# The context tokens' retention gate is computed in the selection stage instead of the output stage

## The reference, cut to what matters

```python
def mixer(h, ...):
    q, k, v, g_ret, cb, cc, cx, ga, gb = jnp.split(h @ w_in, SPLIT_POINTS, axis=-1)
    ...
    y_ret = (jax.nn.silu(g_ret) * o) @ w_ret_o
    u = short_conv3(cc * cx, conv_w)
    y_conv = (cb * u) @ w_conv_o
    merged = jax.nn.sigmoid(ga) * y_ret + jax.nn.sigmoid(gb) * y_conv
    return merged @ w_o, s_f, s_b

def expert_choice_ffn(h, w_router, w_gate, w_up, w_down):
    aff = jax.nn.softmax((hf @ w_router).astype(jnp.float32), axis=-1)
    vals, idx = lax.top_k(aff.T, cap)              # 128 latents, 16 context tokens for each expert
    xs = hf[idx]
    hid = jax.nn.silu(xs @ w_gate) * (xs @ w_up)
    out = (hid @ w_down) * vals                    # added to the rows idx

def trunk_layer(x, cond, ...):
    h = rmsnorm(x, n_pre_mix) * (1.0 + sc1) + sh1
    m, s_f, s_b = mixer(h, ...)
    x = x + g1 * rmsnorm(m, n_post_mix)
    h = rmsnorm(x, n_pre_ffn) * (1.0 + sc2) + sh2
    f = expert_choice_ffn(h, ...)
    return x + g2 * rmsnorm(f, n_post_ffn), s_f, s_b
```

## Time and profile before

| What | Value |
|---|---|
| median of 3 runs | 2033.02 us (2032.63 to 2034.11) |
| the profiled execution's own time | 2034.96 us |
| its span | 2033.2 us |
| mean granted TensorE clock | 0.994 |
| busy share of the span | PE 98%, PEld 83%, DVE 57%, ACT 37%, POOL 13% |

### The profile page before, as it was taken

How to read it: one execution, slowest core, us unless ns; L and a number is a source line. 1 busy time by engine, 2 the same in 40 slices (tenths; PEclk the granted TensorE clock), 3 DMA queues, 4 the chain that set the end, 5 groups by cost and what they waited for, 6 DMA issues and landing times.

```text
span 2033.2 us, 32674 instructions
## 1 busy us (share of the span) xinstructions
PE 1987.5 (98%) x12723; PEld 1694.8 (83%) x12723; DVE 1168.4 (57%) x1621; ACT 753.6 (37%) x869; POOL 272.8 (13%) x277
## 2 busy tenths in 40 slices
PE   6999999999999999999999999999999999999995
PEld 4898989899999999999888888777777777777774
DVE  5654545476554232232223648877777777777766
ACT  7622222231111112111112332655556555555555
POOL 1010101011002000000000122111211111112215
PEclk9999999999999999999999999999999999999998
DMA  9011111225554311112334757788887778888888
GB/s 337 26 53 47 42 46 44 90 83 159 152 152 161 104 33 52 41 32 62 103 93 161 271 180 261 297 318 317 311 310 297 273 299 318 316 316 317 305 312 231
DMA packets 189577, 372.32 MB, mean 183 GB/s; under 512 B 11836, under 2 KB 110132, under 8 KB 188628
## 3 DMA queue, kind: packets, MB, share of 16 engines
q1 hardware_dynamic: 170304, 312.30, 42.4%
q0 software_dynamic: 19120, 59.29, 9.7%
q10 hardware_dynamic: 100, 0.03, 0.0%
HBM read 326.98 MB, written 43.03 MB: 182 GB/s over the span
## 4 chain that ended last, share of the span: by engine, by line
PE 82%; issue 7%; DVE 5%; POOL 2%; DMA 2%; ACT 2%; SPq 0%; POOLq 0%; DVEq 0%; ACTq 0%
PE ps L1436 8%; PE ps L1418 8%; PE ps L1073 8%; PE ps L1074 8%; PE ps L1075 8%; PE ps L1420 8%; PE ps L1427 8%; PE ps L1119 3%; PE ps L1120 3%; PE ps L1121 3%; PE ps L1085 2%; PE ps L1087 2%; PE ps L1086 2%; PE ps L1168 1%; PE ps L1169 1%
## 5 line engine op out<-in xcount | busy, mean ns | idle before, releaser
L2547 DVE TENSOR_TENSOR e_lo<-raw,e_hi 128x2048 fp32r<-128x2048 f32 x192 | 439.2, 2289 | 88.6 <-ACT e_hi L1913 88.6
L1913 ACT CAST e_hi<-raw 128x2048 fp32r<-128x2048 f32 x192 | 367.3, 1913 | 210.8 <-PE ps L1427 209.3
L1073 PE MATMUL ps<-h_hi,w_hi 128*128 128x384 f32 x744 | 249.4, 335 | 0.0
L1074 PE MATMUL ps<-h_lo,w_hi 128*128 128x384 f32 x744 | 248.5, 334 | 0.0
L1075 PE MATMUL ps<-h_hi,w_lo 128*128 128x384 f32 x744 | 248.5, 334 | 0.0
L2100 DVE TENSOR_TENSOR w_lo<-w_raw,w_hi 128x1024 fp32r<-128x1024 f32 x64 | 79.3, 1239 | 192.5 <-ACT w_hi L1612 192.4
L1418 PE MATMUL ps<-e_hi,x_hi 128*128 128x512 f32 x512 | 160.0, 394 | 0.7 <-DVE e_lo L2547 0.4
L1420 PE MATMUL ps<-e_lo,x_hi 128*128 128x512 f32 x512 | 157.8, 389 | 0.0
L1073 PEld LDWEIGHTS ps<-h_hi,w_hi 128*128 128x128 f32 x744 | 139.6, 188 | 3.3 <-issue 3.3
L1074 PEld LDWEIGHTS ps<-h_lo,w_hi 128*128 128x128 f32 x744 | 139.6, 188 | 0.0
L1075 PEld LDWEIGHTS ps<-h_hi,w_lo 128*128 128x128 f32 x744 | 139.6, 188 | 0.0
(11 more groups left out here) (359 smaller groups left out, 3721.2 us busy)
## 6 DMA issues: line engine op xcount, KB each, us to landing
raw<-in_w_gate_dram SPq DMA_DIRECT2D x64, 1024.0 KB, 8.4
raw<-in_w_up_dram SPq DMA_DIRECT2D x64, 1024.0 KB, 13.2
raw<-in_w_down_dram SPq DMA_DIRECT2D x64, 1024.0 KB, 9.6
w_raw<-in_w_in_dram SPq DMA_DIRECT2D x48, 512.0 KB, 4.1
ada_k<-in_w_ada_dram SPq DMA_DIRECT2D x32, 512.0 KB, 5.0
ada<-in_w_ada_dram SPq DMA_DIRECT2D x7, 1024.0 KB, 16.5
merged_d<-merged POOLq DMA_DIRECT2D x8, 576.0 KB, 6.2
ffn_d<-zero POOLq DMA_DIRECT2D x9, 512.0 KB, 7.0
```

The lines of the kernel that those rows point to most:

```text
L1073: pe.matmul(out, w_hi[:, slot, k, :], xh, start=(k == 0), stop=False)
L1074: pe.matmul(out, w_hi[:, slot, k, :], xl, start=False, stop=False)
L1913: act.copy(e_hi[u % 4][:].rearrange("p k n -> p (k n)"), raw[(u + 8) % 12][:].rearrange("p k n -> p (k n)"))\
L2547: dve.tensor_tensor(e_lo[u % 4][:].rearrange("p k n -> p (k n)"), raw[(u + 8) % 12][:].rearrange("p k n -> p (k n)"), e_hi[u % 4][:].rearr ...
```

## The change

- ret_out's gate product is made for latents alone: two blocks of 512 tokens in place of three of 384. The context part of `gate` is filled with 1.0 once, so that w_ret_o's product is stored unscaled for the context.
- CTX_UNITS grows from 8 to 12: units 8 to 11 are the context's ga, in plain float32, with ACT's sigmoid (`sig_ga`) and one more multiplication on POOL. SP loads four more pieces of weights of 1 MB for them. The 22 dummy matmuls go.
- mix_context is cut in pieces: 24 matmuls, 12 matmuls, then 6 and 6 around the flip of the choice.
- DVE's select order: the two m_lo_c subtractions come after rounds 12 and 15 instead of 6 and 8.
- The scaling by the root and by g1, the addition of the input, and the second norm's scaling are now on DVE, behind the first two units of the first expert. h2's transpose, the routing and the choice of the context stand between later units.
- In first_expert TensorE does down units 8 and 9 before the context's units 0 to 7, and the hidden transposes before both.
- SP holds units 3 to 7 of the first expert until the gather of the latents has landed (before, units 5 to 7).
- POOL issues the gather before it makes the context's two roots.

```diff
-CTX_SLOT = [8, 11, 9, 10, 8, 11, 9, 10]
+CTX_SLOT = [8, 11, 9, 10] * 3
...
+            for j in range(4, 8):
+                sp.wait_ge(projected, ctx_made(j))
+                load_ctx(j + 4)
...
+            sp.wait_ge(m_made, NT)
             sp.wait_ge(got_l, 16)
-            for u in range(5, 8):
+            for u in range(3, 8):
                 load_unit(0, u, True)
...
             pool.wait_ge(sel_read, 1)
             gather_latents(0)
+            m_deviation(8, 0)
+            x1_deviation(8, 0)
...
-                for b in range(NB):
+                for b in range(2):
+                    ts = slice(CTX + HALF * b, CTX + HALF * b + HALF)
...
-                    project(T_RETOUT + 2 * n, 0, h_hi, h_lo)
+                    project_latents(T_RETOUT + 2 * n, 0, h_hi, h_lo)
...
-            mix_context(0)
-            mix_context(1)
-            keep_busy(6, 22)
+            pe.wait_ge(act_evicted, EA_CONVOUT + KD + 5)
+            pe.wait_ge(m_lo_done, NT)
+            mix_context(range(0, 4), range(2))
+            pe.wait_ge(m_lo_done, NT + 1)
+            mix_context(range(4, 8), range(1))
...
+            dve.wait_ge(z_lo_done, KD)
+            did(dve.memset(gate[:, 0:CTX], 1.0))
...
-            for half, rounds in enumerate((range(6), range(6, 8))):
+            for half, rounds in enumerate((range(12), range(12, 15))):
...
             def first_expert():
-                dve.wait_ge(ctx_scaled, 2)
-                did(dve.tensor_tensor(h2_own[:], h2_own[:], scale_c[:], ALU.mult))
-                settle()
-                dve.tensor_tensor(h2_own[:], h2_own[:], shift_c[:], ALU.add).then_inc(h2_ready, 1)
                 low(0, 0)
                 low(0, 1)
+                dve.wait_ge(m_rstd, NT)
+                dve.scalar_tensor_tensor(x1_c[:].rearrange("p (a n) -> p a n", a=2), ps[:, 0:2, :], stats[:, 8:9],
+                                         g1_c[:].rearrange("p (a n) -> p a n", a=2), ALU.mult, ALU.mult).then_inc(ctx_scaled, 1)
+                dve.wait_ge(ctx_scaled, 1)
+                dve.wait_ge(xr_in[0], 16 * 5)
+                dve.tensor_tensor(x1_c[:], x1_c[:], x_res_c[:], ALU.add).then_inc(x1_ready, 1)
+                low_rows(0)
+                dve.wait_ge(x1_rstd, NT)
+                dve.scalar_tensor_tensor(h2_own[:], x1_c[:], stats[:, 12:13], scale_c[:], ALU.mult, ALU.mult).then_inc(ctx_scaled, 1)
...
+                low(0, 2)
+                low(0, 3)
+                low(0, 4)
                 top_logit(8)
-                low_rows(0)
+                low(0, 5)
                 affinities(8)
```

More of the change, by code:

```diff
@@ L912, in gather_context @@
                     .then_inc(got_c, 16)
-            pool.wait_ge(m_in[0], 16 * 5)
             for half in range(2):
@@ L1452, in first_expert @@
                         pe.transpose(ps[0:CAP_C, 4, 144:160], sel_f[0:EXPERTS, CAP_L:CAP], id16).then_inc(sel_turned, 1)
[L1453 to L1455 removed]
+                pe.wait_ge(sel_copied, 2)
+                pe.matmul(ps[:, 7, 0:2 * EXPERTS], flip[0:CAP_C, P:2 * P], sel_c[:], start=True, stop=True).then_inc(sel_flipped, 1)
+                for half in range(2):
+                    turn_hidden(half, half + 1)
+                turn_rows(1)
+                down(0, 8)
+                down(0, 9)
                 pe.wait_ge(xc_turned, 1)
```

167 lines of the change are left out of this document (82 added, 85 removed).

## The result

| | before | changed kernel |
|---|---|---|
| median of 20 runs each | 2032.64 us (2030.79 to 2034.37) | 2036.07 us (2033.76 to 2037.64, but for one of 4044.86) |
| the profiled execution's own time | 2034.96 us | 2035.98 us |
| its span | 2033.2 us | 2034.2 us |
| ratio of the runs | 1 | 1.0015, 95% interval 1.0009 to 1.0022 |

The changed kernel is 3.4 us slower, where 1.5 us less than the old median of 2033.02 was forecast. 2036.07 lies in the range of 2026 to 2037.5, but the sign is wrong, and the interval excludes no change. In the profiles the difference is only 1.0 us, since the profiled execution of before (2034.96) was a long one for its kernel. The experiments show where most of that comes from.

A forecast was written before the change was run, and what follows sets the result against it. TensorE, busy 98% of the span, was taken as the bound. The terms -11.3 + 1.0 + 0.1 + 7.2 + 1.5 gave -1.5 us, so 2031.5 us from a median of 2033.02, range 2026 to 2037.5.

The forecast's parts named there:

- Turns 2 to 8 of the retention: Retention's output stage: the gate product in the new form saves 1.61 us a turn, 11.3 us over seven turns.
- The lower bound: Smallest saving for retention turns 2 to 8 if time goes by columns alone: 7 x 1.3 = 9.1 us.
- The first turn: First retention turn: later output transposes delay VectorE, which ends the turn, so it loses 1.0 us.
- The start of the first expert: Selection to first expert: the gathered rows' transposes start where they do now, at 1282.35, so the start moves +0.1 us.
- the 4 us of ctx units that stick out: Selection: of the added 14.46 us of ctx units on TensorE, 4 us exceed the cover of 11.7.
- The gather: POOL's gather beside VectorE's two-input units stands still until unit 0 ends; its rows land at 1282.35.
- The first expert: Context work moved between its units adds 8.4 us, less 1.2 of present waits: 7.2 us more, ends 4 and 10.
- the clock (+1.5): First expert: after a 3.3 us pause, units 0 and 1 meet the lower clock, costing 0.8 to 2.4, taken as 1.5 us.
- The second fall of the clock: Rival: the 2.4 us pause before unit 7 brings half clock there: +2.9, 2034.4 us, chance 0.15.
- The held units: Rival: first expert's held weights arrive together, unit 3 at about 1296 instead of 1287.5: 2038 us, chance 0.12.
- The ctx units' loads: Rival: the selection's four added weight loads are not hidden, TensorE waits up to 3.7 us: 2035 us, chance 0.06.
- signs of being wrong: First expert under 52 us, gate's form saving less than 1.3 us a turn, or unit 3 landing late.

The follow-up runs named there:

- e3: The changed kernel with 7 dummy matmuls before TensorE's wait for the adaLN rows in the first retention turn: median 2035.13 us, ratio 1.0006 to the kernel before.
- e10: The changed kernel with the last output transposes placed earlier between the first turn's gate matmuls, no dummies there: median 2032.64 us, ratio 0.9998 to the kernel before.
- e1: The kernel before, unchanged, profiled a second time: profiled execution 2037.32 us, median 2033.67 us.
- e15: The kernel before, unchanged, profiled a third time: one execution of 2034.0 us.
- e5: e3 with VectorE's context scaling and addition moved in front of the low parts of units 0 and 1: 2034.58 us, ratio 1.0010 to the kernel before.
- e14: e13 with unit 0's low part made during VectorE's wait for the choice's turn, context scaling and addition before unit 1's: median 2029.51 us, ratio 0.9980 to before.
- e8: e3 with unit 7's low part before the context's choice, and the choice's flip between the hidden transposes: median 2032.40 us, ratio 0.9998 to the kernel before.
- e13: The changed kernel with e10's earlier transposes and e8's unit 7 order, no dummies added: median 2031.37 us, ratio 0.9989 to the kernel before.
- e2: The changed kernel, unchanged, profiled a second time: profiled execution 2034.92 us, median 2035.89 us.
- e16: The changed kernel, unchanged, profiled a third time: one execution of 2037.66 us.
- e7: e3 with units 3 and 4 loaded before the gather lands, only 5 to 7 held: median of 9 runs 2037.68 us, ratio 1.0028 to the kernel before.
- e12: The kernel before with 26 dummies instead of 22 under the choice in the selection: median 2032.20 us, ratio 0.9995 to the kernel before.
- e4: The kernel before with only the retention's gate product changed to latents, context's gate left out: median of 5 runs 2023.89 us, ratio 0.9954 to the kernel before.

## Why the prediction was wrong, step by step

- **Turns 2 to 8 of the retention (-11.3).** Right in kind, 1.55 us a turn instead of 1.61: -10.85, which misses by 0.4. The lower bound has a slip: by columns alone the saving is 12.49 - 11.10 = 1.39 us a turn, 9.7 over seven, not 1.3 and 9.1. The measured value lies between the bounds all the same.
- **The first turn (+1.0).** The mechanism was right (transposes late, VectorE late, the turn ends with VectorE) and measures +1.26. The step that failed is what was left out beside it: the price of TensorE's pause, put at nothing without a reason. Both halves of TensorE's wait stood in the text, 1.6 us less product and 1.0 more of VectorE, but they were not added up to a pause of 2.6 us. The text asked what a pause of that length does to the clock in the selection, and not here. The pause was 3.24 us, and the fall behind it costs 1.6 to 1.7 (e3, e10). In place of +1.0 the term is +3.0 where the clock falls, as it did in 3 profiles of 3.
- **The start of the first expert (+0.1).** This is the second step that failed. The term agrees with the first profile, and that is the trap. "A clock of 0.52 where only dummies ran" was taken as free, but the dummies stood in front of the routing, and the 6.24 us of them had set the 1282.35 against which the new rows were compared. Against the usual 47.4 us the changed kernel's 49.0 is +1.6. So the forecast's base held 1.5 us of a fall that was longer in this one of three profiles, and the term was subtracted from a median. That the median's executions mostly have the short fall is not shown; e1 and e15 speak for it. (In the working up to here, the 4 us of ctx units that stick out are 3.3 by the prediction's own rows; its 1272.4 is added up separately and fits: the choice's transposes came 0.9 us later behind the selection's start than before, with 0.7 forecast.)
- **The gather.** Held as forecast (2.48 us, 1.07 when VectorE is idle). The Trainium skill's rule ("GPSIMD Engine Reference", section Specifications), that POOL's memory interface is shared with VectorE and a VectorE instruction with two inputs there gets in its way, agrees with e5 and e14, and with the 0.99 us of the earlier trace rows beside x_lo, a subtraction that takes one of its two inputs from TensorE's output ps.
- **The first expert (+7.2) and the clock (+1.5).** Together 8.7, measured 8.56. TensorE waits 2.47 us for unit 7 (forecast 2.4), 2.17 for the hidden rows and unit 8 (2.4), 0.30 for unit 9 (0.8). But the agreement of the sum is luck. A low clock over units 0 and 1 costs nothing (e8, e13, e14, and e2), since VectorE and the landing of the held weights set unit 7's start; the forecast subtracted only the 1.1 us wait for unit 2 as cover. Its +1.5 made up for two terms that were too small. TensorE's own work in the expert grew by about 2.5 us, not 1.7: in the first profile 55.99 less 4.94 of waits less 1.6 for the fall, against 47.43 less 0.50. And the waits that the expert had before were those 0.5 us, not 1.2. A fall costs where it meets unit 7, which happened in 1 profile of 3 (e16).
- **The sum.** -1.5 + 0.4 + 0.3 + 1.7 + 1.5 - 0.1 = +2.3. The terms are -1.5 forecast, 0.4 for the turns, 0.3 and 1.7 for the first turn, 1.5 for the base, -0.1 for the first expert. The medians show +2.2 in one comparison and +3.4 in the other. What makes up the rest of the 3.4 is open; falls over unit 7 in some executions may be part of it. The stretch between conv and selection, which took 1.3 to 3.8 us more in e1 and e15 than in every profile of after, works against the difference; why ACT's h2T comes late there in some executions is open. What share of the executions of before have no fall in the selection is open too.
- **The rivals.** None came as written. The second fall of the clock was the nearest: it came in e16, behind the pause before unit 7, and cost about 1.4 us there, not 2.9; the pause that decided was in the retention. The held units do not arrive together: unit 3 is in time. But they come one each 4.0 us and not 2.6, so unit 7's weights land 5.3 us later than forecast, and ACT waits for them. In the changed kernel's order that costs little, in e8's it sets the pace. e7 shows that holding only three is worse. The ctx units' loads are hidden; TensorE waited 0.69 for ACT there. None of the prediction's own signs of being wrong appeared: a first expert under 52 us, under 1.3 us a turn, a late unit 3.

## What to carry to other kernels

When one edit shortens the work of an engine and another delays the engine it waits for, add the two: their sum is a new pause, and on TensorE its price is the pause plus what the clock does behind it. A stretch of a trace in which the clock is low is not free because dummies fill it; look what is queued behind them. Take a second profile of the old kernel before a difference of 1 us is read from one. In these runs filling a pause with dummies gave something only where TensorE sets the next step (e3, e12, by their traces). Where another engine does, moving that engine's work gained more (e8, e10, e14), until the next limit, here the landing of held weights.

## What the hardware showed

- A pause of TensorE does not fix whether the clock falls. Behind the wait of 3.2 to 3.3 us in the first turn it fell in 3 profiles of 3, and in e4 behind 3.25 us not at all. Behind 1.66 us (e10) it did not, nor behind 1.7 and 1.8 us (e13, e14); behind 2.05 us in the selection it did in all 4 profiles that had that pause (before, e1, e15, e4). With the pause of 3.2 to 3.5 us before the rows, it fell 1.3 to 1.7 us behind the pause's end in the first profile, e3, e8 and e16, within the pause in e10 and e13, and in e2 only 31 us after the first expert's start. With 1.8 to 1.9 us there (e5, e14) it did not fall at once.
- But for the one at the program's end (16 to 20 us), each fall lasts 3.4 or 6.8 us. One of 3.4 us over TensorE's own path costs half its length, 1.7 us (e3: 1.6); one that a later wait covers costs nothing (the first profile against e2).
- POOL's indirect DMA is issued in 1.07 us beside an idle VectorE (e5, e14), and in 2.48 to 2.49 us beside a two-input subtraction of 2048 columns; a root's small operation beside the same took 1.29 in the changed kernel where it takes 0.20 (e5). e5's second root, beside such work, took 1.61.
- Weights of 1 MB each, asked for right behind the gather's landing, landed 4.0 us apart on average in the changed kernel (unit 3 at 1279.29, unit 7 at 1295.2). With 2 MB asked for beside the gather's issue, the gathered rows came 2.7 us later (e7 against e3).
